# First three up projections by token tile, down and mix products by tile for three units, three rotating half buffers, and another order of work at the borders

## The reference, cut to what matters

```python
# first block, per expert: h = xb @ w_gate_up[e] + b;  glu, lin = halves of h
# act = clamp(glu) * sigmoid(1.702 * glu) * (clamp(lin) + 1);  y = act @ w_down[e] + b
for l in range(2):                                    # second block
    h = rmsnorm(x, norm_mix_pre[l])
    proj = h @ w_in[l]                                # 1024 -> 5888
    ...                                               # three branches, gated: merged
    mix = merged @ w_out[l]                           # 1024 -> 1024
    x = x + rmsnorm(mix, norm_mix_post[l])
    h = rmsnorm(x, norm_ffn_pre[l])
    up = h @ w_up[l]                                  # 1024 -> 5632
    up = conv over 3 neighbouring tokens of up, plus bias
    val, gate = up[..., :2816], up[..., 2816:]
    x = x + rmsnorm((gelu(gate) * val) @ w_down[l], norm_ffn_post[l])
```

## Time and profile before

| | |
|---|---|
| three runs | 2134.41, 2137.47, 2138.20 us; median 2137.47 |
| the profiled execution | 2135.94 us, span 2134.2 us |
| mean granted clock of PE | 0.971 |
| PE busy | 1969.3 us (92%) |
| weight loads busy (PEld) | 1259.7 us (59%) |
| DVE, ACT, POOL busy | 839.3, 696.0, 578.1 us |
| DMA | 609.42 MB, mean 286 GB/s |

### The profile page before, as it was taken

One profiled execution on the slowest core, in us unless ns is written; L12 is line 12 of the kernel. 1 busy time (PEld: TensorE's weight loads), 2 busy tenths in 40 slices (PEclk: granted clock), 3 DMA queues, 4 the chain that ended last, 5 costly groups with the idle time before them and its releaser, 6 DMA issues.

```text
span 2134.2 us, 29440 instructions
## 1 busy us (share of the span) xinstructions
PE 1969.3 (92%) x11433; PEld 1259.7 (59%) x11434; DVE 839.3 (39%) x1323; ACT 696.0 (33%) x1067; POOL 578.1 (27%) x622
## 2 busy tenths in 40 slices
PE   4997799989999999999988889997999999997998
PEld 2874333323333333333322288986998899987997
DVE  3544322211221321122211266417675675256774
ACT  2543211111111111111111246524554556324553
POOL 3400233443342443343344202000242020001340
PEclk8998799999999999999999989998999999998999
DMA  9958699999897999899999945434555554363553
GB/s 355 328 200 346 259 414 417 417 419 413 348 419 295 419 418 418 355 419 417 417 417 419 391 145 178 147 112 162 171 180 180 173 198 128 123 213 100 185 178 131
DMA packets 203048, 609.42 MB, mean 286 GB/s; under 512 B 10458, under 2 KB 115054, under 8 KB 166384
## 3 DMA queue, kind: packets, MB, share of 16 engines
q1 hardware_dynamic: 197360, 585.14, 71.9%
q0 software_dynamic: 5280, 22.19, 3.0%
q10 hardware_dynamic: 328, 0.95, 0.1%
HBM read 607.17 MB, written 9.26 MB: 289 GB/s over the span
## 4 chain that ended last, share of the span: by engine, by line
PE 68%; DMA 10%; DVE 9%; SPq 5%; ACT 5%; issue 3%; POOL 1%; ACTq 0%; DVEq 0%
PE bank L820 31%; PE bank L1120 16%; PE bank L1144 9%; DMA side<-in_w_gate_up 6%; PE bank L1222 3%; SPq L662 3%; SPq L669 2%; PE bank L1071 2%; DVE split L1566 1%; DMA ring<-in_w_down 1%; PE bank L1112 1%; ACT probs L1798 1%; DVE qkv L1544 1%; ACT split L1952 1%; DVE probs L1277 1%
## 5 line engine op out<-in xcount | busy, mean ns | idle before, releaser
L1120 PE MATMUL bank<-ring,qkv 128*64 128x512 f32 x2240 | 499.2, 596 | 25.2 <-POOL ring L2196 25.2
L820 PE MATMUL bank<-hT_hi,split 128*128 128x256 f32 x2368 | 431.9, 285 | 7.4 <-DVE hT_lo L1576 5.8
L820 PEld LDWEIGHTS bank<-hT_hi,split 128*128 128x128 f32 x2368 | 373.1, 194 | 9.9 <-issue 8.1
L1120 PEld LDWEIGHTS bank<-ring,qkv 128*64 128x64 f32 x2240 | 153.3, 137 | 352.8 <-issue 276.4
L1566 DVE TENSOR_TENSOR split<-ring,split 128x2048 fp32r<-128x2048 f32 x112 | 265.7, 2374 | 229.2 <-ACT split L1952 229.1
L820 PE MATMUL bank<-hT_lo,split 128*128 128x256 f32 x1184 | 337.1, 285 | 0.0
L1952 ACT ACTIVATE split<-ring 128x2048 fp32r<-128x2048 f32 x112 | 214.6, 1917 | 369.6 <-PE bank L820 291.0
L1144 PE MATMUL bank<-ring,qkv 128*64 128x512 f32 x1120 | 248.5, 595 | 4.3 <-ACT qkv L1935 3.2
L820 PEld LDWEIGHTS bank<-hT_lo,split 128*128 128x128 f32 x1184 | 229.5, 194 | 0.0
L1541 DVE TENSOR_SCALAR qkv<-bank 128x512 f32<-128x512 f32 x35 | 24.2, 691 | 433.2 <-PE bank L1120 433.2
L2232 POOL TENSOR_TENSOR gated_hi<-probs 128x512 fp32r<-128x512 f32 x22 | 40.8, 1854 | 553.8 <-ACT probs L2082 553.8
(11 more groups left out here) (342 smaller groups left out, 2630.8 us busy)
## 6 DMA issues: line engine op xcount, KB each, us to landing
ring<-in_w_down SPq DMA_DIRECT2D x150, 1024.0 KB, 13.9
ring<-in_w_gate_up SPq DMA_DIRECT2D x70, 1024.0 KB, 17.9
probs<-in_w_gate_up SPq DMA_DIRECT2D x62, 1024.0 KB, 17.7
ring<-in_w_in SPq DMA_DIRECT2D x58, 1024.0 KB, 6.0
ring<-in_w_up SPq DMA_DIRECT2D x44, 1024.0 KB, 5.2
consts<-in_w_gate_up SPq DMA_DIRECT2D x31, 1024.0 KB, 20.5
side<-in_w_gate_up SPq DMA_DIRECT2D x31, 1024.0 KB, 22.4
qkv<-in_w_gate_up SPq DMA_DIRECT2D x31, 1024.0 KB, 21.7
```

Of the source, the lines that this page charges most:

```text
L820: last = pe.matmul(out, a[a_half], b[b_half], start=start and i == 0, stop=stop and i == 2)
L1120: last = pe.matmul(hidden[q][CAP * j:CAP * j + CAP, :], xgT[:, k % 4, k // 4, :], unit_at(k)[:, c:c + 512], start=False, stop=(k == KC - 1 ...
```

## The change

Seven parts.

1. `first_by_tile` (new) makes the first three projections after a norm by token tile. For the inputs (`qa0`, `qa1`, `kv`) that is the order there was, except that PE waits for a tile's second group of turned rows only halfway through the first projection. For up it is new: `val0`, `gate0` and `val1` are made with 128 tokens at a time by `split_project_T_tile` (new), which holds the same 128 x 128 weights and moves 128 columns: 96 matmuls for a unit in place of 48 with 256 columns. Tile 1 is turned before `val1`'s tile 0.
2. mix and down go by tile for their last three units, not two.
3. Up and down halves rotate over three pairs of buffers (0, 1 and the one in `qkv_low`); the four mix units have one pair each. The third mix unit's high half waits for `branch_ready`, since its buffers hold the gates until then. In the up stage a unit's halves are made after the unit three before it has been read by ACT and DVE.
4. Other order at the borders on ACT and DVE (shown below): at mix/up, `up` unit 1's halves come after tile 0's norm, and the turned rows of tile 0 before tile 1's norm. At down/input the next layer's units 0 and 1 are halved between the norms of the two tiles.
5. The load of ACT's table for the root moves from the start of each norm to a place further ahead.
6. In the experts, the last block's scaled high half on ACT (`rows_high`) comes after layer 0's unit 0 is rounded.
7. The linear half of the hidden rows stays in its bank (bank 5) through clamp and product; only the last product writes to SBUF.

The order on PE at the mix/up border of layer 0, before. `hT_hi`, `hT_lo` are the turned rows' halves, `consts,htok` are the transposes; the last number is that of moving columns.

The core of the diff:

```diff
-    slots, owner, holds, turn = {}, {}, {}, 0
+def halves_slots():
+
+    def slot_of(l, u):
+        if u < len(IN2):
+            return u if u < 2 else (2 if l else 3) if u == 2 else (u - 3) % 2
+        return u - FIRST_OUT if u < FIRST_UP else (u - FIRST_UP) % 3
+
+    slots, owner, holds = {}, {}, {}
     for l in range(LAYERS):
         for u in SPLIT:
-            slot = special.get((l, u), turn)
-            if (l, u) not in special:
-                turn = 1 - turn
+            slot = slot_of(l, u)
             owner[l, u], slots[l, u], holds[slot] = holds.get(slot), slot, (l, u)
...
-    for j in range(4):
-        p.tile(f"g{j}")
-    for c in range(UPAIRS):
-        for n in ("val", "gate"):
-            p.bank(f"{n}{c}")
-            p.unit(f"{n}{c}")
+    p.tile("g0")
+    p.tile("g1")
+    p.bank("val0")
+    p.bank("gate0")
+    p.tile("g2")
+    p.tile("g3")
+    p.bank("val1")
+    for n in UP_NAMES[0:3]:
+        p.unit(n)
+    project(UP_NAMES[3:])
...
+            def split_project_tile(b, w_halves, tt, second_group=()):
 
                 for k in range(KC):
+                    if k == KC // 2:
+                        read(*second_group)
                     last = split_product(b[:, tt * 256:tt * 256 + 256], [a[:, k, tt * P:tt * P + P] for a in hT_halves()],
                                          [a[:, k, :] for a in w_halves], k == 0, k == KC - 1)
                 return last
+
+            def split_project_T_tile(b, w_halves, tt, second_group=()):
+
+                tokens = slice(tt * P, tt * P + P)
+                for i in range(2):
+                    for k in range(KC):
+                        if i == 0 and k == KC // 2:
+                            read(*second_group)
+                        last = split_product(b[:, i * T + tt * P:i * T + tt * P + P],
+                                             [a[:, k, i * P:i * P + P] for a in w_halves],
+                                             [a[:, k, tokens] for a in hT_halves()], k == 0, k == KC - 1)
+                return last
+
+            def first_by_tile(prefix, names, product):
+
+                started = {}
+                for tt in range(TT):
+                    groups = [f"{prefix}{2 * tt + g}" for g in range(2)]
+                    for j, n in enumerate(names):
+                        if tt == 0:
+                            if j == 2:
+                                turn_tile(prefix, 1)
+                            started[n] = take(n), next_halves(KC)
+                        if j == 0:
+                            read(groups[0])
+                        last = product(*started[n], tt, groups[1:] if j == 0 else ())
+                        if tt == 1:
+                            used(last)
...
-                read("h0", "h1")
-                started = {}
-                for n in IN2[0:3]:
-                    if n == "kv":
-                        turn_tile("h", 1)
-                    started[n] = take(n), next_halves(KC)
-                    split_project_tile(*started[n], 0)
-                read("h2", "h3")
-                for n in IN2[0:3]:
-                    used(split_project_tile(*started[n], 1))
+                first_by_tile("h", IN2[0:3], split_project_tile)
...
-                split_rows_product("mix", lambda f: (hT_hi[:, f, :], hT_lo[:, f, :]), KC, merged_in, by_tile=2)
-                for tt in range(TT):
-                    turn_tile("g", tt)
-                read(*[f"g{j}" for j in range(4)])
-                for c in range(UPAIRS):
-                    split_project_T(f"val{c}")
-                    split_project_T(f"gate{c}")
-                split_rows_product("down", lambda f: (gated_hi[:, f, :], gated_lo(f)), FT, gated_in, by_tile=2)
+                split_rows_product("mix", lambda f: (hT_hi[:, f, :], hT_lo[:, f, :]), KC, merged_in, by_tile=3)
+                turn_tile("g", 0)
+                first_by_tile("g", UP_NAMES[0:3], split_project_T_tile)
+                for n in UP_NAMES[3:]:
+                    split_project_T(n)
+                split_rows_product("down", lambda f: (gated_hi[:, f, :], gated_lo(f)), FT, gated_in, by_tile=3)
...
-                own(dve.tensor_scalar(lin, banks[5][:, :], -SWIGLU_LIMIT, SWIGLU_LIMIT, ALU.max, ALU.min))
+                linear = banks[5][:, :]
+                own(dve.tensor_scalar(linear, linear, -SWIGLU_LIMIT, SWIGLU_LIMIT, ALU.max, ALU.min))
                 dve.wait_ge(clamped, i + 1)
-                own(dve.scalar_tensor_tensor(out=lin, in0=lin, scalar=1.0, in1=glu, op0=ALU.add, op1=ALU.mult))
+                own(dve.scalar_tensor_tensor(out=linear, in0=linear, scalar=1.0, in1=glu, op0=ALU.add, op1=ALU.mult))
                 dve.wait_ge(sig_ready, i + 1)
-                dve.tensor_tensor(act_row, lin, sig, ALU.mult).then_inc(act_ready, 1)
+                dve.tensor_tensor(act_row, linear, sig, ALU.mult).then_inc(act_ready, 1)
...
-                    layer_rows("down", 1, gpost2[1])
+                    take_low(l, 0)
                     state["l"] = l
                     hT_low("h", 0, c_pre)
+                    take_low(l, 1)
                     state["l"] = l - 1
+                    layer_rows("down", 1, gpost2[1])
                     layer_scaled("down", 1, layer_in)
-                    take_low(l, 1)
...
+                take_low(l, FIRST_UP + 1)
+                hT_low("g", 0, c_ffn)
                 layer_rows("mix", 1, gpost2[0])
                 layer_scaled("mix", 1, x_mid)
-                hT_low("g", 0, c_ffn)
+                take_low(l, FIRST_UP + 2)
                 normed(1, x_mid)
                 hT_low("g", 1, c_ffn)
-                take_low(l, FIRST_UP + 1)
...
-                        take_low(l, FIRST_UP + 2 * (c + 1) + half)
...
+                        take_low(l, FIRST_UP + 2 * c + half + 3)
+                take_low(l, *range(FIRST_DOWN + 3, N_UNITS))
...
+            def rows_high(i):
...
+            activations(0)
+            with act.Fori(1, n_blocks) as i:
+                rows_high(i - 1)
+                activations(i)
...
-                    act.activation(spare, eps, ACT.Sqrt)
...
+            act.activation(spare, eps, ACT.Sqrt)
+            act.wait_ge(hidden_done, n_blocks)
+            take_high(0, 0)
+            rows_high(n_blocks - 1)
...
-                    act.activation(spare, eps, ACT.Sqrt)
                     act.wait_ge(tile_rows, seen(tile_rows))
                 else:
...
-                    layer_squares("down", 1)
+                    take_high(l, 0, 1)
                     state["l"] = l
                     turn_high("h", 0, c_pre)
+                    state["l"] = l - 1
+                    layer_squares("down", 1)
                     post_root(1)
-                    take_high(l, 1)
                     pre_root(1, layer_in)
...
-                take_high(l, *range(FIRST_OUT, FIRST_UP + 2))
+                act.activation(spare, eps, ACT.Sqrt)
+                take_high(l, FIRST_OUT, FIRST_OUT + 1)
+                act.wait_ge(branch_ready, 2 * (l + 1))
+                take_high(l, FIRST_OUT + 2, FIRST_OUT + 3, FIRST_UP)
                 layer_squares("mix", 0)
                 post_root(0)
                 pre_root(0, x_mid)
+                take_high(l, FIRST_UP + 1)
+                turn_high("g", 0, c_ffn)
                 layer_squares("mix", 1)
                 post_root(1)
-                turn_high("g", 0, c_ffn, (0,))
+                take_high(l, FIRST_UP + 2)
                 pre_root(1, x_mid)
-                turn_high("g", 0, c_ffn, (1,))
...
-                        take_high(l, FIRST_UP + 2 * (c + 1) + half)
...
+                        take_high(l, FIRST_UP + 2 * c + half + 3)
...
-                take_high(l, *range(FIRST_DOWN + HALVES, N_UNITS))
-                if l + 1 < LAYERS:
-                    take_high(l + 1, 0)
+                act.activation(spare, eps, ACT.Sqrt)
+                take_high(l, *range(FIRST_DOWN + 3, N_UNITS))
...
```

15 lines of the change are left out of this document (5 added, 10 removed).

## The result

Before and changed kernel, four executions each on one chip: 2137.84 us (2134.41 to 2139.21) and 2170.22 us (2167.61 to 2171.53). The ratio is 1.0149, 95% interval 1.0131 to 1.0167. The forecast was 2146 us, with a range of 2124 to 2157: the sign was right, the size and the range were not. The profiled execution has a span of 2168.5 us and a mean clock of 0.965 (before: 2134.2 and 0.971), so 34.3 us are to be found.

The account below looks back on a forecast made before the run. Experts bound by DMA, the second block's layers by PE. Terms: mix/up +13.6, experts -3.8, their end -0.3, down -2.3, down/input +1.8, sum +9.0 us: 2144.9 from the profiled 2135.9, 2146 against the runs; range 2124 to 2157.

Parts of the forecast that it names:

- The faster rival: Up by tile: load hidden behind the matmul, columns decide; 2125 at 0.080 us a matmul, about 2113 at 0.060; chance 0.22.
- x: Up by tile: time of one 128-column matmul, taken as 0.117 us, between 0.113 and 0.120.
- The mix/up border in layer 0: Mix to the end of up's three units by tile: up starts 9.0 us earlier before clock loss; net +6.8 us a layer.
- the stall: In mix, PE waits 2.8 us for the third unit's high half, held by `branch_ready`.
- the 0.8 put on the clock: Mix/up border: gaps of 2.8 and 2 us may bring the low clock; 0.8 us added, half such a spell's least cost.
- the 33.7 forecast: Up's three units by tile: 288 matmuls of 128 columns at 0.117 us, 33.7 us a layer where it was 17.3.
- The experts: Blocks before the double block: PE's wait for DVE's line 1544 goes, -3.8 us, between 0 and -5.
- their end: End of the experts: +0.8 for unit 0's earlier rounding, -1.1 for waiting on one group of turned rows; sum -0.3 us.
- Down's stall: Down: with three pairs of buffers the stall of 1.13 us a layer goes, -2.3 us, between 0 and -2.3.
- The term, +1.8: Down/input border: `qa0` 1.8 us sooner, but tile 1's rows and `kv` later; +1.8 us, between 0 and +4.
- That mechanism: Much slower rival: clock stays at 1.2 GHz through up's three units, 33.7 us a layer, up to 2213; chance 0.07.
- its next smaller case: Much slower rival, up's three units: the low clock for one short stretch, some 10 us, 2156.

Follow-up runs that it names:

- the timed kernels: Tenth to twelfth up projections in two 128-column passes, ratio 1.0101, against the kernel with up whole and the border as before, ratio 0.9964.
- the edit alone: The kernel before with only the experts' linear half left in its bank: 2131.20 us, ratio 0.9977.
- the timed pair: Up whole, border as before, with three up projections in two 128-column passes: tenth to twelfth 2156.72 us, first three 2218.91 us.
- two others: Changed kernel with up whole in layer 1 alone (profiled 2175.63 us), or with 96 added matmuls ahead of layer 1's stream (profiled 2182.24 us).
- the fill: Changed kernel with overwritten 256-column matmuls, 16 in the 2.05 us gap and 22 misplaced outside the mix stall: 2148.56 us, ratio 1.0050.
- both kernels that had them: Overwritten matmuls added to the changed kernel (2148.56 us), and to the kernel with up whole and the border as before (2123.25 us).

## Why the forecast had the sign and not the size

- The price of a matmul with 128 columns, 0.117 us from the earlier trace rows, was right in kind and a little high: 0.110 in a long window of the changed kernel, 0.111 from the timed kernels, against 0.120 with 256. Halving the columns saved 0.009 us, so they don't set the pace; that the load does is argued from its records, and no run varied it. The faster rival, which needed x under 0.101, did not come about.
- The mix/up border in layer 0: the stall came within 0.1 us, and up began 1.0 us later than forecast (29.6 against 28.6 after the start of mix), since the stall's own low spell took 1.6 and the 0.8 put on the clock was too little for it. The stream then took about 1.7 us less than the 33.7 forecast. So +6.1 against +6.8 is near in part by luck.
- The experts: -3.8 forecast, -4.1 with their end; -4.9 (-2.8 to -7.3) timed for the edit alone, -4.2 in its trace. The cause was the one named, the operand read from a bank.
- Down's stall went (-2.3 forecast in all, -1.4 in each layer measured). At the down/input border the forecast had `qa0` 1.8 us sooner and the price on `kv`; measured, `qa0` itself is 1.8 us later, by the wait for its bank. The term, +1.8, was met by luck.
- **The step that failed** is "The gaps of 2.8 and 2 us may bring the low clock, as the 2.91 did; I add 0.8, half of what such a spell has cost at least". It took the price of a low spell from a stream of 256 columns, 1.7 to 2.3 us, and used it for another stream. The runs show a spell's length to hang on what runs in it: under 256-column matmuls the clock rose 3.8 to 6.0 us after the first of them (spells of 13.7 and 17.1 us with the gaps before), under 128-column ones it rose only after the stream's end. One caught layer costs 28.2 us more than forecast (33.9 less the 5.65 of the sum), and less the 2.3 by which layer 0 starts sooner than forecast (6.4 against 4.1) and 0.6 of smaller terms this is the whole of what was missing, 34.3 less 9.0 = 25.3 us.
- That mechanism stood among the rivals, with its price, 33.7 us a layer, about right (31 by the timed pair, 28 in the trace). It was given 0.07 and its next smaller case was called a short stretch, some 10 us. The executions show the case between, one whole stream, as the usual one. The wrong chance had a plain root: no row of before had a 128-column stream at the lower clock, so nothing spoke against the rival, and nothing was written against it. A cost that no row bounds belonged in the range, and the range ended at 2157.

By the rows, 232 matmuls with 128 columns in 49 us without a gap stayed at 0.50, while 256-column matmuls behind the gaps of this border came back to 1.00 within 6.0 us. The Trainium skill, "TensorE: Matmul & The Clock Gate", Part 1 (The HAM clock gate), has sustained work of the engine bring the upper clock back. The rows with 256 columns agree with it and those with 128 do not, though PE is busy 49.00 of 49.00 us. By the Trainium skill's page the loss would have been a short one, like the forecast's 0.8 us.

Open: what decides in one execution whether the clock falls behind a gap of 2.05 us. The layer that was caught differs between kernels (layer 1 in two profiles of the changed one, layer 0 in two others), and for one kernel the executions differ. By their times, nine of ten executions of the changed kernel had just one caught layer and none had none, so it does not look like a separate toss for each layer. That the fall needs the idle time is shown by the fill. Whether it needs the 128-column matmuls behind the gap as well is not shown: the same gap ahead of 256-column ones left the clock at 1.00 in both layers of its one profiled execution, and this was not tried further.

## What to carry to other kernels

Do not price a split of the moving dimension by its columns alone: with a fresh load of 128 fp32r columns for each matmul, going from 256 moving columns to 128 took 0.120 us to 0.111 and doubled their number. Do not put such a stream right behind a gap of the tensor engine: once the clock was low it stayed so to the stream's end, and the 288 matmuls cost 46 us more than the form with 256 columns, where the same stream after dense work cost 15 more. Where a gap can't be closed, matmuls that compute nothing, put inside it, held the clock here in both kernels that had them; and when executions of one program fall in clusters, read the granted clock before anything else.

## What the runs showed of the hardware that was not expected

- A gapless stream of fp32r matmuls with 128 moving columns and a load each stayed at 1.2 GHz for 61 to 75 us, in all six traced cases: two found it low, and in four it fell 2.3 to 2.6 us after the stream began. It rose 2.4 to 3.5 us after the last of them began. With 256-column ones the spells at this border were 13.7 to 17.1 us. At 2.4 GHz the same stream kept the clock (286 matmuls in 32 us at 1.00).
- One program, one chip, two clusters 25 to 30 us apart (2140 to 2145 and 2165 to 2176), by mean clocks of 0.970 to 0.973 and 0.957 to 0.963; the traced execution of the slower one has the low spell behind a gap of 2.05 us.
- Gaps as short as 2.1 to 2.8 us were followed by the lower clock, not every time: a stall of 2.8 us in mix brought 3.4 us of it in layer 0 and none in layer 1 of one execution.
- A 128-column matmul with its load took 0.110 to 0.112 us at the upper clock and 0.211 at the lower; one with 256 takes 0.120 at the upper, and has the same record of 415 ns at the lower.
- Useless matmuls inside the three gaps of the mix/up border made it no longer and gave 2.5 us a layer in matmuls done; 22 put outside a gap cost 2.6 us a layer.
